# Modulation inside the DeltaNet heads in two groups of four units instead of four couples

## The reference

```python
mod = cond @ w_mod + b_mod                       # 6 x 1024 values, shifts, scales and gates
h   = rmsnorm(x) * (1 + scale1) + shift1
p   = h @ w_in                                   # one projection for all three mixers
o_a = gated_deltanet(p...)                       # 4 heads, forward and backward, in chunks
o_b = differential_attention(p...)               # 4 heads
o_c = hyena(p...)
x   = x + gate1 * (merge(o_a, o_b, o_c) @ w_out)
x   = x + gate2 * swiglu(rmsnorm(x) * (1 + scale2) + shift2)
```

## Time and profile before

| | us |
|---|---|
| median of three runs (lowest, highest) | 3254.38 (3253.41, 3256.84) |
| the profiled execution | 3254.38 |
| its span, first to last instruction | 3252.6 |
| PE busy / DVE / ACT / POOL | 3020.7 / 1388.2 / 781.2 / 1442.5 |

### The profile page before, as it was taken

How to read it: one execution, slowest core, us unless ns; L and a number is a source line. 1 busy time by engine, 2 the same in 40 slices (tenths; PEclk the granted TensorE clock), 3 DMA queues, 4 the chain that set the end, 5 groups by cost and what they waited for, 6 DMA issues and landing times.

```text
span 3252.6 us, 54706 instructions
## 1 busy us (share of the span) xinstructions
PE 3020.7 (93%) x20800; PEld 2824.1 (87%) x20800; DVE 1388.2 (43%) x2240; ACT 781.2 (24%) x1607; POOL 1442.5 (44%) x1106
## 2 busy tenths in 40 slices
PE   6999999999989999999989999999999999999997
PEld 6988888777969999999989888887788789999997
DVE  3167675554745231121151677645565542212112
ACT  2233432333122120000113333324422311101011
POOL 1475555322415434444445655542333153544443
PEclk8999999999999999999989999999999999999998
DMA  5212222333225112222221122232222231222221
GB/s 213 72 67 95 72 71 90 121 127 112 93 64 185 59 59 71 75 74 72 92 98 65 58 85 95 72 107 88 86 81 96 94 138 52 78 69 74 71 73 70
DMA packets 79697, 287.12 MB, mean 88 GB/s; under 512 B 8322, under 2 KB 8324, under 8 KB 77572
## 3 DMA queue, kind: packets, MB, share of 16 engines
q1 hardware_dynamic: 77616, 274.17, 24.9%
q10 hardware_dynamic: 1588, 9.10, 0.8%
q0 software_dynamic: 288, 1.05, 0.1%
HBM read 253.35 MB, written 30.93 MB: 87 GB/s over the span
## 4 chain that ended last, share of the span: by engine, by line
PE 76%; DVE 10%; POOLq 4%; issue 3%; DVEq 2%; ACT 1%; POOL 1%; DMA 1%; ACTq 0%; SPq 0%
PE ps_G L751 36%; PE ps_GPM L751 23%; POOLq L2403 2%; DVE outs L1914 2%; PE ps_GPM L849 2%; DVE outs L2037 2%; PE ps_M L878 1%; POOLq L2468 1%; DVE outs L2014 1%; PE ps_M L1142 1%; PE ps_M L1167 1%; PE ps_M L1017 1%; PE ps_M L1240 1%; POOLq L2401 1%; PE ps_M L1033 1%
## 5 line engine op out<-in xcount | busy, mean ns | idle before, releaser
L2400 POOL CAST w_hi<-ring 128x1024 fp32r<-128x1024 f32 x304 | 322.3, 1060 | 1565.3 <-PE ps_G L751 702.6
L2402 POOL TENSOR_TENSOR w_lo<-ring,w_hi 128x1024 fp32r<-128x1024 f32 x304 | 755.0, 2484 | 45.4 <-issue 1.0
L751 PE MATMUL ps_G<-x_hi,w_hi 128*128 128x320 f32 x1728 | 559.4, 324 | 27.4 <-POOLq L2403 12.4
L751 PE MATMUL ps_G<-x_hi,w_lo 128*128 128x320 f32 x1728 | 538.9, 312 | 0.0
L751 PE MATMUL ps_G<-h_lo,w_hi 128*128 128x320 f32 x1600 | 499.8, 312 | 0.0
L751 PEld LDWEIGHTS ps_G<-x_hi,w_hi 128*128 128x128 f32 x1728 | 330.3, 191 | 40.0 <-issue 21.5
L751 PE MATMUL ps_G<-room_o,w_hi 128*128 128x320 f32 x1248 | 328.1, 313 | 12.6 <-DVE room_o L1867 6.7
L751 PEld LDWEIGHTS ps_G<-x_hi,w_lo 128*128 128x128 f32 x1728 | 329.4, 191 | 0.0
L751 PE MATMUL ps_GPM<-room_o,w_hi 128*128 128x320 f32 x1248 | 324.9, 311 | 0.0
L751 PEld LDWEIGHTS ps_G<-h_lo,w_hi 128*128 128x128 f32 x1600 | 306.4, 191 | 1.9 <-issue 1.9
L751 PE MATMUL ps_G<-room_a,w_hi 128*128 128x320 f32 x960 | 223.6, 322 | 36.7 <-POOLq L2403 36.7
(11 more groups left out here) (416 smaller groups left out, 5781.5 us busy)
## 6 DMA issues: line engine op xcount, KB each, us to landing
ring<-in_W SPq DMA_DIRECT2D x384, 512.0 KB, 3.6
big<-projected_tiles SPq DMA_DIRECT2D x12, 1280.0 KB, 6.9
projected_tiles<-big SPq DMA_DIRECT2D x40, 320.0 KB, 4.4
projected_tiles<-outs SPq DMA_DIRECT2D x32, 320.0 KB, 4.4
big<-in_MODS SPq DMA_DIRECT2D x4, 2048.0 KB, 22.1
big<-projected_tiles SPq DMA_DIRECT2D x18, 320.0 KB, 5.2
x<-in_X SPq DMA_DIRECT2D x2, 2560.0 KB, 10.2
big<-in_FWD ACTq DMA_DIRECT2D x2, 1632.0 KB
```

Of the source, the lines that this page charges most:

```text
L751: m = pe.matmul(ap, w[wi][:, k, n0:n0 + width], acts[ai][k][:, a:b], start=(k == 0 and i == 0), stop=(k == chunks - 1 and i == 2))
L2400: nc.gpsimd.tensor_copy(hi, raw)
L2402: nc.gpsimd.tensor_tensor(wlo[:, slot * UNIT:(slot + 1) * UNIT], raw, hi.bitcast(F32), ALU.subtract)
```

## The change

The eight units of modulation of a DeltaNet head are used in two groups of four instead of four groups of two. To have four of them in the ring at once, the order of the kinds becomes w w m m m m w m m m m w. Group (0 to 3) stands in level 3 of the inverse, group (4 to 7) behind step 1 of the state. The fillers move: job 2a goes from levels 3 and 4 to levels 5 and 6, job 3a from step 1 to the end of the head, ahead of job 3b. ACT's copies and POOL's splits follow: POOL now splits units 0 and 1 at the start, unit 6 behind the scaled keys and ahead of the masks of level 5, and unit 11 behind the masks of level 6, still ahead of the decay products of the next head. Number and size of units, jobs, loads and products are the same.

```diff
 def stream(layer):
-    return [..., ("delta", H, "wmm" * 4), ...
+    return [..., ("delta", H, "wwmmmmwmmmmw"), ...
...
 @block.tensor
                     job("delta", 0, "b", L, hd)
-                    mod_units("delta", (0, 1), L, hd)
                     job("delta", 1, "a", L, hd)
                     for lev in range(1, NLEV):
...
-                        if lev <= 4:
-                            job("delta", *((1, "b"), (2, "a"))[(lev - 1) // 2], L, hd, (range(0, 4), range(4, KC))[(lev - 1) % 2])
+                        if lev in (1, 2, 5, 6):
+                            job("delta", *((1, "b"), (2, "a"))[lev // 4], L, hd, (range(0, 4), range(4, KC))[(lev - 1) % 4 % 2])
+                        if lev == 3:
+                            mod_units("delta", (0, 1, 2, 3), L, hd)
...
-                        if lev == 2:
-                            mod_units("delta", (2, 3), L, hd)
...
-                    gap_half = [(2, "b"), (3, "a")]
                     for step in range(4):
...
-                        if step < 2:
-                            job("delta", *gap_half[step], L, hd, range(0, 3))
+                        if step == 0:
+                            job("delta", 2, "b", L, hd, range(0, 3))
...
                         if step == 1:
-                            mod_units("delta", (4, 5), L, hd)
+                            mod_units("delta", (4, 5, 6, 7), L, hd)
...
+                    job("delta", 3, "a", L, hd)
                     job("delta", 3, "b", L, hd)
-                    mod_units("delta", (6, 7), L, hd)
...
 @block.gpsimd
                     split("delta", [0], L, hd, -5)
-                    split("delta", [3], L, hd, 0)
+                    split("delta", [1], L, hd, 0)
...
-                    for lev in range(3):
+                    for lev in range(5):
                         level(lev)
-                    split("delta", [6], L, hd, 1)
-                    level(3)
-                    level(4)
...
                     pool.drain().then_inc(kd_ready.sem, 1)
+                    split("delta", [6], L, hd, 1)
                     level(5)
                     level(6)
-                    split("delta", [9], L, hd, 4)
+                    split("delta", [11], L, hd, 2)
                     if hd < H - 1:
                         decay_products(hd + 1)
...
-                    split("attn", ws[:1], L, hd, -3 if hd == 0 else ...
-                    split("attn", ws[1:2], L, hd, -2 if hd == 0 else ...
+                    split("attn", ws[:1], L, hd, -5 if hd == 0 else ...
+                    split("attn", ws[1:2], L, hd, 0 if hd == 0 else ...
```

More of the change, by code:

```diff
@@ L49, in stream @@
 def stream(layer):
-    return [("A", 3, "wwww"), ("Z", 1, "wwww"), ("delta", H, "wmm" * 4), ("attn", H, "wwmmwwmm" if layer < DEPTH - 1 else "wwww"),
+    return [("A", 3, "wwww"), ("Z", 1, "wwww"), ("delta", H, "wwmmmmwmmmmw"), ("attn", H, "wwmmwwmm" if layer < DEPTH - 1 else "wwww"),
             ("C", 3, "wwww"), ("G", 1, "wwww"), ("mix", 3, "wwww"), ("out", 2, "wwww"),
@@ L1075, in _ @@
                             pe.matmul(ap[:, 0:P], XT[:, 4 * d + c, :], rr[:, d, :], start=True, stop=True).then_inc(fl, 1)
-                        if step < 2:
-                            job("delta", *gap_half[step], L, hd, range(3, 6))
+                        if step == 0:
+                            job("delta", 2, "b", L, hd, range(3, 6))
                         for d in range(2):
@@ L1085, in _ @@
                             m.then_inc(fl, 1)
-                        if step < 2:
-                            job("delta", *gap_half[step], L, hd, range(6, KC))
+                        if step == 0:
+                            job("delta", 2, "b", L, hd, range(6, KC))
                         if step == 0:
@@ L1528, in _ @@
                             act.drain().then_inc(p_ready.sem, 1)
-                        if lev in (2, 4):
-                            job("delta", *((1, "b"), (2, "a"))[lev // 4], L, hd)
+                        if lev == 2:
+                            job("delta", 1, "b", L, hd)
                         if lev in (3, 5) and hd < H - 1:
@@ L1538, in _ @@
                         act.drain().then_inc(vn_ready.sem, 1)
+                    job("delta", 2, "a", L, hd)
                     for j in range(3):
@@ L1554, in _ @@
                             silu(2, hd + 1)
-                        if step < 2:
-                            job("delta", *((2, "b"), (3, "a"))[step], L, hd)
+                        if step == 0:
+                            job("delta", 2, "b", L, hd)
                     table(ACT.Sqrt)
@@ L1565, in _ @@
                     act.drain().then_inc(orms.sem, 1)
+                    drained("delta", "rows1", L, hd, 10)
+                    copy_rows(mod_rows if hd < H - 1 else mod_rows_b, rows_delta.sem)
+                    job("delta", 3, "a", L, hd)
                     job("delta", 3, "b", L, hd)
-                    drained("delta", "rows1", L, hd, 11)
-                    copy_rows(mod_rows if hd < H - 1 else mod_rows_b, rows_delta.sem)
                 act.wait_ge(head_done.sem, head_done.at(L, 0) * H + H)
@@ L2495, in _ @@
                     vc = pr("v_ctx").rearrange("p (i n) -> p i n", i=H)[:, hd, :]
-                    split("attn", ws[:1], L, hd, -3 if hd == 0 else ws[2] - len(PHASE_AT[L, "attn"][2]) + 1)
-                    split("attn", ws[1:2], L, hd, -2 if hd == 0 else ws[3] - len(PHASE_AT[L, "attn"][2]) + 1)
+                    split("attn", ws[:1], L, hd, -5 if hd == 0 else ws[2] - len(PHASE_AT[L, "attn"][2]) + 1)
+                    split("attn", ws[1:2], L, hd, 0 if hd == 0 else ws[3] - len(PHASE_AT[L, "attn"][2]) + 1)
                     if hd == 0:
```

## The result

The changed kernel takes **3341.8 us** (median of four runs, 3329.8 to 3345.5), the kernel before 3255.6 us in the runs beside it: a ratio of 1.026, 95% interval 1.023 to 1.0285, so it is 2.6% slower. The forecast was 3334, its range 3296 to 3362. The profiled execution took 3340.9 us with a span of 3339.1, 86.5 us more than before.

What follows compares the result with a forecast made beforehand. PE is 92% busy, but DVE's chain bounds levels 1 to 5 and POOL's ordered queue the next head's start. Six heads at +12.4 us (+74) and two last heads (+5) on 3254.4 give 3334 us, range 3296 to 3362.

Steps and rivals of the forecast that it cites:

- Couple (0,1): Ahead of level 1: the couple goes, PE then waits for a POOL mask; gain 0.6 us, bounds 0 and 1.96.
- Levels 2 to 4: Couple (2,3) and job 2a's halves leave, one four enters, all beside DVE's chain; costed at nothing.
- Levels 5 and 6: Unit 6's split delays level 5's masks and job 2a's halves stand there; +4.2 us, bounds 0 to 5.3.
- Step 1: Step 1 of the state: job 3a leaves, the modulation starts after 5.2 instead of 6.17 us; gain 1.0.
- The tail and its clock: Head's end: next head's decay products wait behind unit 11's late load and split, +8.3 us; half clock, +1.5.
- The clock: Clock halves after PE gaps over 4 us; mostly covered by waits, 1.5 us taken per head with a successor.
- rival C: Clock stays low through job 0a and beyond, 3.5 us per head, load takes 5.5: 3358 us; chance 0.09.
- Last heads: Each layer's last head, without successor: fillers and small waits outweigh gains; +2.5 us each, bounds -1 and +4.5.
- Sum: Six heads with a successor at +12.4 us make +74, two last heads +5: 3334 us; chance 0.70.
- Rival A: Next head's first products don't wait for POOL's chain; 31 us of PE work come through: about 3223 us; chance 0.06.
- B: Rival: tail as forecast, but job 2a hides in levels 5 and 6 and the clock holds: about 3296 us; chance 0.10.
- D: Rival: fours from the ring don't run side by side as the first ones do: 3365 us; chance 0.02.

Runs made afterwards that it cites:

- run 1: Changed kernel with the next head's decay products ahead of POOL's split of unit 11; 3288.7 us, ratio 1.0104.
- run 2: Changed kernel with POOL's scaled keys behind the masks of levels 5 and 6; 3338.6 us.
- run 11: Changed kernel with decay products ahead of unit 11's split, keys behind masks, unit 6's split behind level 5's masks; 3279.8 us.
- run 8: Kernel before with only the second four (job 3a at the end), decay products ahead of unit 11's split; 3257.1 us.
- run 5: Changed kernel with decay products ahead of unit 11's split, keys behind levels 5 and 6's masks, job 2a whole at level 4's end; 3254.6 us, profiled once.
- run 12: The same kernel as run 5, timed; 3260.3 us, ratio 1.0013.
- run 10: Changed kernel with decay products ahead of unit 11's split, keys behind masks, taps 6 to 8 to level 5, 9 to 11 to level 6; 3255.0 us.

## Why the prediction was right

The times stand in us behind job 0a of the same head, so that a late head does not count twice; the second head of the first layer, as in the prediction.

- **Couple (0,1): forecast -0.6, measured -0.5** to level 1's second products (20.15 instead of 20.68), and -0.66 in run 1, where job 0a runs at full clock.
- **Levels 2 to 4: forecast 0, measured -0.7.** Level 4's first products come at 39.79 instead of 41.05, 1.26 earlier, of which 0.5 are the couple (0,1). DVE is still the chain there, but one tap of it (line 1912) takes 0.72 us instead of 1.58. Without the split ahead of it, the mask that the tap meets runs 1.36 us earlier, and in both kernels the tap ends 0.35 us behind that mask. I had left out that moving POOL's split moves POOL's masks against DVE's taps.
- **Levels 5 and 6: forecast +4.2 with bounds 0 to 5.3; near by luck in part.** The state's first products come 4.16 later (68.02 instead of 63.86); with the 1.26 won ahead of level 4's products taken off, levels 4 to 6 lose 5.4. The forecast counted from today's times, so each of its links can be held against job 0a: masks of level 5 +3.72 (forecast 3.8), end of its first products +1.63 (1.5), its second products +3.47 (3.3), level 6's first products +2.89 (2.9), its second products +4.17 (4.2). The mechanism was the one named (keys and split ahead of the masks, half of 2a on the path). The luck is in POOL's queue: it starts the keys 1.26 us earlier than the forecast let it, and then takes 0.85 longer from the keys to the split (7.19 us instead of 6.34 to the masks; the keys meet DVE's taps) and 0.41 longer for the split (4.13 instead of 3.72). And the forecast took the 0.6 ahead of level 1 off once more (-0.6 + 0 + 4.2 = +3.6), though its wait for the masks, counted from today's times, already swallows it. Two things were not seen: the stretch at half clock behind the 5.20 us, and that DVE would have been late by itself with the masks on time (run 2).
- **Step 1: forecast -1.0, measured -1.07** (5.10 us instead of 6.17 up to the group).
- **The tail and its clock: forecast +8.3 and +1.5, measured +9.36 together.** From PE's first product behind the second group (385.39; 368.57 before) to the next job 0a it takes 25.34 us instead of 15.98, made of: issue 0.22, landing 3.67, 0.18 for POOL to take it, split 3.53, 0.27, decay products 13.52 (12.8 in the earlier trace rows), 0.29, split of unit 0 3.56, 0.10. That is the forecast's chain link by link, and it alone makes up the time. The decay products are longer because two of their instructions take 0.92 and 0.91 us instead of 0.60, the two that meet DVE's products of two SBUF tensors (line 1982). So the 1.5 set down for the clock was not paid there: what is over the 8.3 is POOL's. The half clock costs job 0a itself 0.10 us in this head and 0.85 in the third (3.62 and 4.37 us instead of 3.52). The predicted second wait ahead of job 0a, some 2 us, is nearly gone (0.28 us) because the first products, at half clock, fill it, and the first is 5.82 us instead of 4 to 5. Run 1 puts 53 us, or 8.8 per transition, on this chain.
- **The clock.** The Trainium skill's rule against idle gaps between bursts (page "TensorE: Matmul & The Clock Gate", section "Why this matters for your kernels") agrees with what ran: 0.50 behind gaps of 5.82, 5.20, 4.47 (run 1) and 3.00 us (run 11). But its strict reading, rival C, did not come: at a head's start the slow stretch fell into the wait for unit 0's split, as the forecast said. In level 5 it was not foreseen. The second fours at half clock in runs 2, 8 and 11 stand behind gaps of only 1.59 us; what decided there stays open.
- **Last heads: forecast +2.5 each, measured +5.9 and +4.0** (99.3 and 99.1 instead of 93.4 and 95.0). Here the step failed: I let PE come to level 5's second products at about the same time as in the earlier trace rows, with the two halves of 2a behind that, and counted no clock. In the first layer PE waits 3.71 us for the masks of that level, then works at 0.50 through its first products, and with a half of 2a in front the second products come 4.4 us late (55.40 instead of 51.02). Run 2, with the masks early, takes 3.4 and 3.8 us of it back, run 5 all of it (92.6 us in both).

```profile
570.66 2.08 PE L1016 MATMUL ps_M<-outs 128*128 128x128 f32 x8 [3.71 <-POOLq L2468]
```

- **Sum:** the six transitions, from job 0a to job 0a, cost 75 us (forecast 74), the last heads 10 (forecast 5): +85 of the span's 86.5, where +79 was forecast. Rival A (the 31 us come through) was wrong at the place I named, the first products of each head; B missed what the levels lose; D falls by the fours of 1.95 us. The chain was the right one, but that the sum for a head came so near has some luck in it: the 1.5 us set down for the clock stand where POOL's chain was 1.1 longer than counted.

What stays open: why run 12's times spread over 17 us (3251.4 to 3268.4) when those of the kernel before spread over 8. In the two executions of this kernel that were profiled (runs 5 and 12, spans 5.8 us apart) it is not the heads: from the first job 0a to the last they differ by 0.8 us in the first layer and 0.1 in the second, but by 3.8 ahead of the first head and by 4.6 between the layers' heads. Run 10 was executed once, and its taps were not tried together with run 5's filler. And a ring of more than four units, which would free unit 11 from the second four, was not tried.

## What to carry to other kernels

Work that is taken off the busiest engine is worth only what it was worth in the places where it stood. Here one couple stood beside DVE's chain, one ahead of a wait for a mask, and what the other two gave back was used up by a job that lost its cover: 29 us less of PE's work (run 10) did not shorten the span. In an engine that takes its program in order, ask of every instruction that waits for a late transfer what is queued behind it: moving one call (the split of the last unit) behind another gave back 53 of 86 us. And a filler belongs where its engine waits for another one that is busy anyway; moved two levels on, it stood in the chain, while its old cover became an idle gap that also cost the clock.

## What the runs showed of the hardware that was not expected

- DVE's taps and POOL's instructions took turns, whole instructions at a time: a tap of 0.89 us takes 2.31 when it meets a split's subtraction of 2.36 us, 1.73 when it meets a mask. Beside POOL's keys, short instructions of 0.60 us each, it keeps its 0.89, and the key that meets it takes 1.27 instead.
- Where a tap was moved decided which engine was late: with 3 taps one level on, level 5 came 4.4 us earlier (run 10), and the split that now ran beside a subtraction and a transpose of level 4 (0.42 and 0.45 us, as elsewhere) slowed neither.
- The granted clock was 0.50 behind a gap of only 3.00 us (run 11), although DVE was busy for 4.26 and POOL for 4.49 of the 5.10 us ahead of it.
- Behind a gap of 1.59 us the granted clock was 0.52 in one head of run 8 and 1.00 in the next, though the 5.6 us ahead look alike in the trace (PE busy for 3.77 and 3.78 us). At half clock the same four takes 3.53 us instead of 1.95. The rows do not tell what decides it.
